# Two-layer decoder with grouped experts: a ninth weight slot, a new place for the crowded pairs, and another order inside each pair

## The reference, cut to what matters

```
for i in range(DEPTH):                     # 2 layers
    mix = moba_attention(x, ...) if i % 2 == 0 else nsa_attention(x, ...)
    x = layer_norm(DEEPNORM_ALPHA * x + mix, ln_g[i, 0], ln_b[i, 0])
    ffn = grouped_moe(x, router_w, router_b, moe_w_gate[i], moe_w_up[i], moe_w_down[i])
    x = layer_norm(DEEPNORM_ALPHA * x + ffn, ln_g[i, 1], ln_b[i, 1])

# grouped_moe, for each expert e and the tokens xt that chose it (two experts each, of one group of four):
hid = silu(xt @ w_gate[e]) * (xt @ w_up[e])      # 1024 -> 512
out[tokens] += weight * (hid @ w_down[e])        # 512 -> 1024
```

## Time and profile before

| | us |
|---|---|
| median of 3 runs | 1276.44 |
| lowest, highest | 1274.03, 1276.81 |
| the profiled execution | 1276.07 |
| its span, first to last instruction | 1274.3 |

### The profile page before, as it was taken

The page is one execution under the profiler, slowest core; times in us unless marked ns, Lnnn a source line. Parts: engine busy times, 40 slices in busy tenths (PEclk is TensorE's granted clock), DMA queues, the critical chain, the costliest instruction groups (busy, mean ns, idle before and its releaser), DMA issues. The chain is left out here.

```text
span 1274.3 us, 17802 instructions
## 1 busy us (share of the span) xinstructions
PE 1044.0 (82%) x7482; PEld 572.9 (45%) x7482; DVE 291.2 (23%) x842; ACT 174.8 (14%) x440; POOL 40.7 (3%) x106
## 2 busy tenths in 40 slices
PE   8999999998666668657899899899996676676775
PEld 6675444444333335323588654444453343243332
DVE  0016431112111111111311685321211211111112
ACT  0014310110000000000121462211010000000000
POOL 2001010000000000000000120100000000000000
PEclk9999999999878878888999999999997888788788
DMA  9933659999999999999995305599999999999994
GB/s 329 402 155 133 231 222 417 404 426 427 427 427 427 427 428 428 426 428 423 383 315 202 129 2 221 216 410 404 427 426 427 427 426 428 427 427 427 428 426 191
DMA packets 51568, 450.93 MB, mean 354 GB/s; under 512 B 3915, under 2 KB 10284, under 8 KB 25884
## 3 DMA queue, kind: packets, MB, share of 16 engines
q1 hardware_dynamic: 49136, 442.51, 83.9%
q0 software_dynamic: 2016, 6.81, 1.6%
q10 hardware_dynamic: 332, 0.40, 0.1%
HBM read 448.63 MB, written 1.07 MB: 353 GB/s over the span
## 5 line engine op out<-in xcount | busy, mean ns | idle before, releaser
L787 PE MATMUL bank<-ring,work 128*32 128x256 f32 (+1 forms) x2688 | 261.5, 493 | 117.5 <-DMA ring<-in_moe_w_up 70.5
L787 PEld LDWEIGHTS bank<-ring,work 128*32 128x32 f32 (+1 forms) x2688 | 126.0, 136 | 251.8 <-issue 229.0
L1301 DVE TENSOR_TENSOR work<-work,bank 128x256 f32<-128x256 f32 (+1 forms) x32 | 15.6, 488 | 592.3 <-PE bank L787 592.3
L787 PE MATMUL bank<-bias,work 128*32 128x256 f32 (+1 forms) x448 | 95.9, 538 | 52.8 <-DMA softmax_area<-in_moe_w_gate 31.7
L598 PE MATMUL bank<-xT,ring 128*128 128x256 f32 x448 | 99.1, 381 | 0.7 <-ACT xT L1538 0.7
L787 PE MATMUL bank<-softmax_area,work 128*32 128x256 f32 (+1 forms) x448 | 95.9, 539 | 0.0
L787 PEld LDWEIGHTS bank<-bias,work 128*32 128x32 f32 (+1 forms) x448 | 44.4, 148 | 104.8 <-issue 100.6
L598 PEld LDWEIGHTS bank<-xT,ring 128*128 128x128 f32 x448 | 84.4, 190 | 13.5 <-issue 1.4
L1309 DVE TENSOR_TENSOR acc<-acc,bank 128x512 f32<-128x512 f32 x120 | 76.6, 684 | 33.1 <-PE bank L853 25.6
L836 PE MATMUL bank<-ring,work 128*32 128x512 f32 x576 | 73.7, 654 | 6.2 <-DMA ring<-in_moe_w_down 5.3
L762 PE MATMUL bank<-xT,work 128*128 128x256 f32 (+1 forms) x384 | 76.4, 354 | 1.2 <-DVE xT L1270 1.2
(11 more groups left out here) (211 smaller groups left out, 935.8 us busy)
## 6 DMA issues: line engine op xcount, KB each, us to landing
ring<-in_moe_w_gate SPq DMA_DIRECT2D x48, 2048.0 KB, 28.3
ring<-in_moe_w_up SPq DMA_DIRECT2D x44, 2048.0 KB, 28.8
ring<-in_moe_w_down SPq DMA_DIRECT2D x44, 2048.0 KB, 28.8
bias<-in_moe_w_down SPq DMA_DIRECT2D x8, 2048.0 KB, 21.6
softmax_area<-in_moe_w_down SPq DMA_DIRECT2D x8, 2048.0 KB, 26.5
bias<-in_moe_w_gate SPq DMA_DIRECT2D x8, 2048.0 KB, 24.5
softmax_area<-in_moe_w_gate SPq DMA_DIRECT2D x8, 2048.0 KB, 29.1
bias<-in_moe_w_up SPq DMA_DIRECT2D x8, 2048.0 KB, 28.0
```

The lines of the kernel that those rows point to most:

```text
L787: last = mm(bank[2 + k][row:row + cap, 0:width], xgT[:, t, at + e * cap:at + (e + 1) * cap], w[e][:, t, part * width:(part + 1) * width], ...
L1301: v.tensor_tensor(hid[:, 0:n], silu[:, 0:n], bank[3][:, 0:n], ALU.mult).then_inc(hid_ready[l], 1)
```

## The change

1. **Ninth slot.** The third load of pair 1 (its first up weight) gets a slot of its own, made of `work[:, 0:2048]` and of `xT`. Its first half is issued once all attention scores have been read, its second once the router product is done. For that `xsP` moves from `work` to `acc`, the running sum (`total`) is kept in `xs`, `hid` overwrites `silu`, and `pick` takes the old place of `hid`. The loads behind it shift by one slot: pair 1's second up and first down weight now come in halves behind `gate_half`.
2. **Crowded pairs.** The wide pairs are 0, 1, 8 and 9; the most crowded sorted experts are taken in pairs 8 and 9. `GROUPS` has seven entries in place of six.
3. **Order in a pair.** `transpose_hidden` and `down` come straight after `gate_up`; then the weight transposes (into bank 3, no longer bank 7), the scatter of the pair before, and both parts of the next gather. The last pair keeps its order.
4. **Layer 2 projections by token tiles.** Groups 0 and 1 are computed as four blocks of 128 tokens (`first_tiles`): tile 0 of group 0 before tile 1 is transposed.
5. **Idle products.** The two at the start and the two between the layers are gone; one of 256 columns is put ahead of the first gather of each layer.

```diff
-WIDE, CAP_WIDE, CAP_NARROW = 4, 64, 32
+WIDE_PAIRS, CAP_WIDE, CAP_NARROW = (0, 1, 8, 9), 64, 32
-GROUPS = [(0, 1, CAP_WIDE), (1, 1, CAP_WIDE), (2, 2, CAP_WIDE), (4, 4, CAP_NARROW), (8, 4, CAP_NARROW), (12, 4, CAP_NARROW)]
+GROUPS = [(0, 1, CAP_WIDE), (1, 1, CAP_WIDE), (2, 2, CAP_NARROW), (4, 4, CAP_NARROW), (8, 2, CAP_WIDE), (10, 4, CAP_NARROW), (14, 2, CAP_NARROW)]
...
-        xsP = work[:, 0:2048].rearrange("p (k t d) -> p k t d", k=NT, t=KT)
+        xsP = acc[:, :, :].rearrange("p k (t d) -> p k t d", t=KT)
+        total = xs
-        hid = work[:, 5120:5632]
+        hid = silu
-        pick = xT[:, 0:2, :].rearrange("p a b -> p (a b)").rearrange("p (t s) -> p t s", t=NT)
+        pick = work[:, 5120:5632].rearrange("p (t s) -> p t s", t=NT)
...
+        spare_parts = [work[:, 0:2048], xT[:, :, :].rearrange("p t q -> p (t q)")]
+        def in_spare(key):
+            return key[0] == "pair" and key[2:] == (1, 2)
...
+                if slot_no(u) == SPARE_SLOT:
+                    sp.wait_ge(scores_read[l], len(job_pairs[l]))
+                    sp.dma_start(spare_parts[0].rearrange("p (t n) -> p t n", t=KT // 2), src[:, 0:KT // 2, :]).then_inc(loaded[SPARE_SLOT], 16)
+                    sp.wait_ge(logits_ready[l], 1)
+                    sp.dma_start(spare_parts[1].rearrange("p (t n) -> p t n", t=KT // 2), src[:, KT // 2:KT, :]).then_inc(loaded[SPARE_SLOT], 16)
+                    return
...
             def gather(l, g, part):
                 if part == 0:
+                    if g == 0:
+                        keep_warm(1, 256)
                     pe.wait_ge(pick_ready[l], g + 1)
...
                     gate_up(l, i)
+                    transpose_hidden(l, i)
+                    down(l, i)
+                    if i < PAIRS - 1:
+                        weights_by_slot(l, i)
                     if 0 < i < PAIRS - 1:
                         spread(l, i - 1)
-                    transpose_hidden(l, i)
                     if more:
-                        gather(l, group_of[i] + 1, 0)
-                    if i < PAIRS - 1:
-                        weights_by_slot(l, i)
-                    down(l, i)
-                    if more:
-                        gather(l, group_of[i] + 1, 1)
+                        for part in range(2):
+                            gather(l, group_of[i] + 1, part)
...
-                keep_warm(2)
                 pe.wait_ge(first_loaded[0], 16)
...
-            for tt in range(NT):
-                normed(0, 1, tt)
-                transpose_x(2, tt)
-                if tt + 1 < NT:
-                    keep_warm(2)
-            xT_here(2, NT - 1)
...
-            for g in range(3):
-                nsa_group(g)
+            def first_tiles(tt, g):
+                w = nsa_slot(slot8, 0)
+                for n in range(2):
+                    for t in range(KT):
+                        last = mm(bank[g][:, n * SEQ + tt * P:n * SEQ + (tt + 1) * P], tile_cols(2 * g + n)(w, t),
+                                  xT[:, t, tt * P:(tt + 1) * P], start=(t == 0), stop=(t == KT - 1))
+                return last
+            normed(0, 1, 0)
+            transpose_x(2, 0)
+            arrived(1, 0)
+            xT_here(2, 0)
+            first_tiles(0, 0)
+            normed(0, 1, 1)
+            transpose_x(2, 1)
+            first_tiles(0, 1)
+            xT_here(2, 1)
+            for g in range(2):
+                first_tiles(1, g).then_inc(proj_ready[1], 1)
+            nsa_group(2)
```

131 lines of the change are left out of this document (77 added, 54 removed).

## The result

The changed kernel takes 1265.96 us (median of 4 runs, 1265.44 to 1267.41) against 1275.24 for the kernel before (4 runs, 1273.42 to 1276.81): a ratio of 0.9932, with a 95% interval of 0.9911 to 0.9953. The same kernel in a later session gave 1265.33 (6 runs) and 0.9921 (0.9894 to 0.9948). The forecast was 1264 in a range of 1258 to 1270.5. By the medians the gain is 9.3 us; the forecast had 12.1. The profiled execution of after took 1266.07 us, with a span of 1264.3.

A forecast was written before the change was run, and what follows sets the result against it. Expert stages were taken as bound by weight transfers at 427 GB/s, with engine chains ahead of them. Gains of 7.8 + 1.6 + 1.5 + 1.2 = 12.1 us from 1276.4 gave 1264 us, range 1258 to 1270.5.

The forecast's parts named there:

- both stages: Expert stages: ninth slot, down block first and narrow pairs 2 and 3 save 3.9 us a layer, 7.8 in all.
- transition: Between the layers: projecting by token tiles starts earlier and gains 1.2 us, bounds -1 and 1.4.
- start: Kernel start: removing two idle products lets the first projections begin earlier, gaining 1.6 us, bounds 0 and 3.1.
- ahead of the gather: Layer 0's first gather: one idle product keeps the clock up, gaining 1.5 us, bounds -0.5 and 1.6.
- the forecast of 597: End of layer 0's expert stage: its last up weight lands near 597 us.
- the 1.5 to 3 that I had named as a sign: Start of layer 0's expert stage: the first freed load goes out 1.5 to 3 us earlier than 172.56.
- Last pair: End of each stage: pair 14's later scatter delays the last gates but just fits; 0 us, bounds +2 and -2.
- Wide pairs 8 and 9: Mid-stage: PE falls about 4 us behind, narrow pairs regain it, no queue hole; 0 us, bounds 0 and 3.
- rival 3: Wide pairs 8 and 9 run at the lower clock throughout: +23 us a layer, 1310 us; chance 0.04.
- Rival 2: Fewer idle products: no start gain, layer 0's gather fall stays, another comes at the transition; gain 7.5, 1269 us; chance 0.10.
- Rival 1: Pairs 0 to 2 give the lead back; each layer keeps 1.5 us, total gain 7.3, 1269 us; chance 0.16.
- rival 4: Ninth load not hidden, SP held on a wait past 172 us; each layer keeps about 0.7, 1271 us; chance 0.03.

The follow-up runs named there:

- a: The kernel before with only the ninth slot added, plus the buffer moves it needs; ratio 0.9987.
- after_again: The changed kernel, unaltered, run again in a later session; 1265.33 us, ratio 0.9921.
- f: The changed kernel with pairs 0 to 3 wide as before, ninth slot and new order kept; ratio 1.0029.
- i: The changed kernel with the two idle products at the start back and none ahead of the first gather; 1264.53 us, ratio 0.9926.
- e: The changed kernel without the ninth slot; ratio 0.9975.
- j: The changed kernel with pair 14 scattering pair 13 ahead of its own hidden transposes; 1266.97 us, ratio 0.9953.
- l: The changed kernel with three idle products of 512 columns added in layer 1's attention; 1262.56 us, ratio 0.9922.
- Kernels a to d: The kernel before with, in turn, the ninth slot, the moved wide pairs, the new order, and all three; ratios 0.9987, 0.9968, 1.0022, 0.9916.
- g: The changed kernel with the old order inside a pair, ninth slot and wide pairs 8 and 9 kept; ratio 0.9958.
- m: The changed kernel with the edits of i, j and l together; 1264.35 us, ratio 0.9929.

## Why the prediction was right, point by point

The time was right to 2 us (1264 against 1265.96). The largest term was right for the reason given; that the whole came so near was in part luck, for the stages and the transition gained 1.9 us more than forecast, two small terms together 1.8 less, and a loss of 2.1 us that I had not named came on top. In us gained, by the two profiled executions:

| term | predicted | profile | what the runs add |
|---|---|---|---|
| both stages | 7.8 | 8.9 | the account closes in eight of nine rows |
| transition | 1.2 | 1.95 | 1.95 wherever the clock held |
| start | 1.6 | 0.9 | 0.2 lost on the mean of 14 profiles, about 1 either way |
| ahead of the gather | 1.5 | 0.35 | the term is wrong |
| layer 1's attention | not named | -2.1 | falls of the clock |
| sum | 12.1 | 10.0 | |

**Ninth slot, order and narrow pairs.** The step by step working held. I had 4.4 us of holes, and the rate gives 4.1; 3.4 before was read off directly. Pair 1's down block ended 50.4 us behind the first gate product (about 50), the hop to ScalarE cost 0.68 (0.7), and the sentence that the slot alone would gain nearly nothing is run a. The last ups start 427.4 us behind the first freed load; the forecast of 597 behind a freed load at 169.5 was 427.5. In absolute time they start at 598.7, since the lead-in was late: the first freed load went out 1.28 us earlier, just short of the 1.5 to 3 that I had named as a sign. In layer 1 the ups start 2.6 us earlier (431.8 to 429.2), not 3.9.

**Last pair.** Put at 0 with bounds of 2 on both sides. TensorE slipped by about as much as it had waited before (2.41), and the wait for the last up weight vanished. That brought 0.6 us in layer 0 (behind the ups the stage took 12.3 us in place of 12.9) and 1.7 in layer 1 (11.4 in place of 13.1). The up block no longer follows a wait at the lower clock (in before the granted clock was 0.50 from 604 to 607 us and for 3.4 us from 1248.9); against that stands 1.8 us in layer 1 in which TensorE came later than the load (429.2 against 427.4 in after_again). This is where the stages' extra 1.1 us come from.

**Wide pairs 8 and 9.** Zero was right, with no hole and the clock at 1.00; rival 3, and with it the worry that the waits would slow them, is out. TensorE waits for transfers again from pair 9's up block on.

**Transition.** The mechanism was right and the size low. I took 14.9 us for four blocks and 1.0 for the transposes. From 619.57 to 634.84 they took 15.3 together, since blocks follow each other at 3.6 us where I had used the 3.73 of a group's own length. The 0.15 held back for the copy of the first bank was not needed. Removing the two idle products there was usually free; in f and i the clock fell and took 1.6 back.

**Start: the step that failed.** "Useful products would run at half speed until about the same moment" was half right: they did, and the second group started at nearly the same time. The half of 3.1 us that I took was a mean between bounds; the lower bound was the answer. What I had not seen is that the idle products sometimes run at full speed, in i and a. There the second group starts at 25.6 and 25.8 us; in e, j and l, where TensorE was as fast just before but had no idle products, a fall of 3.4 us came at 11.3 to 12.4 us and the second group starts at 27.0 to 27.3.

**Idle product ahead of the gather: the step that failed.** I tied the gather's fall to its 0.77 us of waiting, since layer 1 had 0.40 and none. Run i waits 0.76 us and has no fall; after has 0.25, and the fall sits in the router product 10 us earlier. Kernels a to d wait 0.76 or 0.77 us there and have no fall either. So the wait alone does not bring the fall; what does stays open.

**The clock elsewhere.** Rival 2 was the right kind of thing at the wrong place: it charged the clock with falls at the gather and the transition, while the one that cost most is in code that the change doesn't touch. Of the eleven profiles of changed kernels without idle products there, ten have it (g has its fall in the router product behind it), and before hasn't, so the kernel before had something to lose there that its own profile couldn't show. Rival 1 (1.5 us a layer left) didn't come; nor did rival 4, since the second half of the ninth load went out at 157.23, 14 us ahead of the first freed load.

## What to carry to other kernels

Extra prefetch in front of a stage is worth its bytes only if the consumer frees buffers early enough; work it out as bytes saved less new idle time of the queue, and look for the edits (less work early in the stage, the freeing block ahead of the others) that the buffer needs. An edit that costs time alone may be the one that pays when another is there, so one-at-a-time trials would have rejected two of the three here. Idle products that keep the clock up should be judged on several profiles of several kernels, since the falls lay at the same places in two profiles of one kernel and moved from kernel to kernel, and a single comparison can't tell an edit's effect from that.

## What the runs showed of the hardware that I had not expected

- The granted clock fell to 0.50 for 3 to 7 us in TensorE work with gaps of only 0.3 to 1.8 us (713 to 720 us in after, with 6.47 of 7.00 us busy), and with three idle products ahead of the transposes it was absent in both kernels that have them (l and m). The Trainium skill (TensorE: Matmul & The Clock Gate, section "A second HAM failure mode: psum-queue depth-cycling") tells, for bf16 products, of small idle times between groups of products that make the clock swing. This trace, in float32, agrees with its gaps of 1.83 and 0.53 us; the kernel before has the same gap of 1.83 and held its clock at 1.00, so the gaps alone don't settle it.
- At the start the same idle products took 3.78 us in before and 1.98 in i, and the granted clock says 1.00 in both: these slow products at the start don't show in it. It is the duration of a known product (the table product, 1.46 against 0.83 us) that tells. Falls a little later do show (in e, j and l, at 11.3 to 12.4 us).
- The lag from the first freed load to the landing of the last ups repeats to 0.9 us in six stages of four profiles (427.0 to 427.9), the transition to 0.02 us where the clock holds, while whole runs of one kernel spread over 2 to 10 us (1259.41 to 1269.56 in after_again). Stretches between fixed instructions resolve what medians can't.
